# The copy of a relative bias to HBM, in one piece from GpSimd or head by head behind the weights

## The chip, the cores and the metric

One core of one Trainium2 chip. The metric is the device time of one execution in microseconds. Three runs of the kernel before gave 1661.22, 1663.39 and 1664.31 us; the profiled execution is a fourth one.

## What is computed

The reference is two layers of one kind of block, then one layer of another, on 256 tokens of width 1024, all in float32. A layer of the first kind is a mixer (windowed attention, dense attention and a gated branch), cross attention to a memory, and a feed-forward with a convolution over the tokens:

```
def conv_ffn(x, w_up, conv_k, conv_b, w_down):
    h = x @ w_up                                   # 1024 -> 2 * 2816
    h = sum(hp[:, j:j + S] * conv_k[j] for j in range(CONV_W)) + conv_b
    a, b = jnp.split(h, 2, axis=-1)
    return (jax.nn.gelu(a, approximate=False) * b) @ w_down
```

The second block's attention has 16 heads and adds to its scores a bias that depends on the distance of query and key alone, `bias_gr[:, :, t5_bucket(dist_w)]`. Its table is made early: for each head one row of 384 values over the distance, with a large negative number where the key lies ahead of the query.

## The kernel before

**Weights.** All weights lie in one stream in HBM, in the order of use. Each is multiplied as two parts of reduced precision: ScalarE rounds a raw piece into a buffer `wh` (L998), VectorE subtracts that from the raw piece and leaves the rest in `lows` (L1503), and TensorE makes three products of the parts (`run`, L478). Pieces of equal form are loaded two at a time, one group to a DMA: in the feed-forward a group is 128 partitions by 2048 values, 1 MB. The buffer `raw` is a ring of NR = 4 groups; `wh` has NH = 6 buffers, and the two casting engines go at most LA = 3 pieces ahead of the piece that is about to be multiplied. SyncE does nothing but issue these transfers (`sync`, L2354): before group gi it waits until TensorE has used group gi - 4. The queue of SyncE holds nothing else.

**The feed-forward.** There are NZ = 22 steps n. Step n takes two pieces, the features n and n + 22, which are one group: 24 matmuls of 128x256 each. ScalarE moves each product out of PSUM with scale and bias (L1243), VectorE adds the two neighbours of the convolution (L1833, L1836), ScalarE applies Gelu (L1225), GpSimd multiplies the halves (`e.tensor_tensor(hc...)`, L2275), ScalarE and VectorE split the product in two parts (L1228, L1823). Four PSUM banks go round among these products. Then the down-projection takes 22 pieces of 128x1024, 11 groups, 12 matmuls of 128x512 for each.

**The bias.** In layer 0 the selection matrix is loaded into `PT` once the cross attention has read `PT` for the last time (L1220). After feed-forward step 4 one matmul makes the table (L781), and VectorE adds the mask and writes `PT[0:16, 1024:1536]`, one head to a partition, in step 6 (L1842, signal `rel`). The copy to the scratch tensor `d_scr` [16, 128, 384] in HBM repeats each head's row 128 times, because the reader in the second block takes row p with an offset that shrinks by one from partition to partition (L2306). GpSimd issues the copy as one DMA behind its product of step 7 (L2278). The signal `bias_out` counts its end. In layer 1, `PT` is written again, by ScalarE (L1126) and VectorE (L1712), which wait for `bias_out`; GpSimd waits for it before it loads the table (L2304).

**Other DMAs.** GpSimd also loads parameters and gains; the 1.2 MB of parameters of layer 1 go out behind its last product of layer 0's feed-forward (L2281).

Of the kernel before, what the change touches and what calls it, by code (L numbers as in the profile page):

```python
# [231 lines left out]
def build(nc, wstream, specs_out, cst_d, rel_d, par_d, par2_d, x_d, xT_d, memT_d, lnp_d, scr_d, out_d, layout):  # L232
    with ExitStack() as ctx:

        def sb(name, f):
            return ctx.enter_context(nc.sbuf_tensor(name, [128, f], F32))
# [4 lines left out]
        def signal(name, step=1):  # L241
            s = Signal(ctx.enter_context(nc.semaphore("s_" + name)), step)
            signals.append(s)
            return s
# [8 lines left out]
        vec = signal("vec")  # L253
# [3 lines left out]
        cst_in, x_in, p2_in, rel_in, mem_in, bias_out, bias_in = (  # L257
            signal(n, 16) for n in ("cst", "x", "p2", "rel", "mem", "bias_out", "bias_in"))
# [16 lines left out]
        PT = sb("PT", 2048)  # L275
# [26 lines left out]
        def arena(n):  # L302
            o = at[0]
            at[0] += n
            assert at[0] <= ARENA
            return ar[:, o:o + n]
# [35 lines left out]
        def pr(name, p=128):  # L342
            o, n = layout["par"][0][name]
            return par[0:p, o:o + n]
# [16 lines left out]
        up = arena(RN * 259).rearrange("p (n t) -> p n t", t=259)  # L361
# [53 lines left out]
        pieces = Pieces()  # L415
# [32 lines left out]
        def unit(un):  # L448

            return un // 4, un // 2 % 2, un % 2, 4 * (un % 2)  # L450
# [536 lines left out]
        def scalar(e):  # L987
            w = Waits(e)
# [37 lines left out]
            for l in range(DEPTH):  # L1026
# [90 lines left out]
                def probs_copied(un):  # L1117
                    br, i, hh, hold = unit(un)
                    w.wait_ge(cross, "pT", l, un, 0)
                    if un < 2:  # L1120
                        if l:
                            w.wait_ge(bias_out)
                            w.wait_ge(cross, "xpv", l - 1, un)
                    else:
                        w.wait_ge(cross, "pv", l, un - 2)
                    e.copy(PTv[:, hold:hold + 2, :, :],  # L1126
                           A["pT", l, un, 0][:, :].rearrange("p (h k q) -> p h k q", h=2, k=2)).then_inc(*act.done("pT", l, un, 0))
# [124 lines left out]
                if l + 1 < DEPTH:  # L1252
# [3 lines left out]
                    n = pieces.of["kv", l + 1][-1] + 1  # L1256
# [16 lines left out]
            n = pieces.of["q2", 0][-1] + 1  # L1273
# [221 lines left out]
        def vector(e):  # L1495
            w = Waits(e)
# [57 lines left out]
            for l in range(DEPTH):  # L1554
# [148 lines left out]
                def probs_copied(un):  # L1703
                    br, i, hh, hold = unit(un)
                    w.wait_ge(cross, "pT", l, un, 1)
                    if un < 2:
                        if l:
                            w.wait_ge(bias_out)
                            w.wait_ge(cross, "xpv", l - 1, un)
                    else:  # L1710
                        w.wait_ge(cross, "pv", l, un - 2)
                    e.tensor_copy(PTv[:, hold + 2:hold + 4, :, :],  # L1712
                                  A["pT", l, un, 1][:, :].rearrange("p (h k q) -> p h k q", h=2, k=2)).then_inc(*vec.done("pT", l, un, 1))
# [112 lines left out]
                for n in range(NZ):  # L1826
                    for half in range(2):
                        m = n + half * NZ
                        lows_for("up", l, m)
                        h = hc[:, (2 * n + half) % 8, :]  # L1830
# [20 lines left out]
                if l + 1 < DEPTH:  # L1851
# [3 lines left out]
                    n = pieces.of["kv", l + 1][-1] + 1  # L1855
# [26 lines left out]
            n = pieces.of["q2", 0][-1] + 1  # L1882
# [135 lines left out]
            for i in range(2):  # L2018
# [4 lines left out]
                first = soff + 31  # L2023
# [160 lines left out]
        def gpsimd(e):  # L2184
            w = Waits(e)
# [10 lines left out]
            def scaled(tag, *ready):  # L2196

                w.wait_ge(*ready)
                for i in range(2):
                    e.tensor_scalar(xt(i), xt(i), ALPHA, None, ALU.mult).then_inc(*pool.done("scaled", *tag, i))  # L2200
# [23 lines left out]
            for l in range(DEPTH):  # L2224
                scaled((l, 1), *((x_in,) if l == 0 else (cross, "xT", 0, 3, 1, 1)))

                def rope_sin(br, i):
                    Xv = qk[:, i, 640 * br:640 * br + 640].rearrange("p (h s d) -> p h s d", s=2, d=32)
                    t2v = room[br][:, 640:1280].rearrange("p (h s d) -> p h s d", s=2, d=32)
                    n1 = rot[:, br, i, 32:64].unsqueeze(1).to_broadcast([128, 10, 32])  # L2230
                    if i:
                        w.wait_ge(vec, "rope", l, br, 0)
                    e.tensor_tensor(t2v[:, :, 0, :], Xv[:, :, 1, :], n1, ALU.mult).then_inc(*pool.done("sin", l, br, i))

                w.wait_ge(cst_in)
                if l:
                    for n in range(NZ - 4, NZ):
                        w.wait_ge(pool, "z", 0, n)
                        w.wait_ge(vec, "z", 0, n)
                for i in range(2):  # L2240
                    w.wait_ge(act, "q", l, 0, i)
                    w.wait_ge(act, "k", l, i)
                    rope_sin(0, i)
                for i in range(2):
                    w.wait_ge(vec, "vvar", l, i)
                    inverse_root(sm[:, 32 * i + 15:32 * i + 16], sm[:, 32 * i + 14:32 * i + 15]).then_inc(*pool.done("vrs", l, i))
                    w.wait_ge(vec, "qvar", l, i)
                    inverse_root(sm[:, 84:94], sm[:, 74:84], 10).then_inc(*pool.done("qrs", l, i))
                    if i == 0:
                        w.wait_ge(vec, "qg", l, 0)  # L2250
                        rope_sin(1, 0)
                    w.wait_ge(act, "vn", l, i)
                    w.wait_ge(par_in[l])
                    e.tensor_tensor(vt[:, i, :], vt[:, i, :], pr("clng"), ALU.mult).then_inc(*pool.done("vgain", l, i))
                    w.wait_ge(pool, "vgain", l, i)
                    e.tensor_tensor(vt[:, i, :], vt[:, i, :], pr("clnb"), ALU.add).then_inc(*pool.done("vn", l, i))
                w.wait_ge(vec, "qg", l, 1)
                rope_sin(1, 1)
                for kind, n, d in fills:
                    if kind == "merge" and n != 2:  # L2260
                        w.wait_ge(vec, "mul", l, n, d)
                        w.wait_ge(*((vec, "mul", l, 2, d) if n == 0 else (pool, "merged", l, 0, d)))
                        e.tensor_tensor(merged[:, d, :], merged[:, d, :], gates[:, gate_at[n] + d, :],  # L2263
                                        ALU.add).then_inc(*pool.done("merged", l, n, d))
                normed((l, 1))
                next_gains((l, 1), 3 * l + 1, (l, 2))
                scaled((l, 2), cross, "xT", l, 1, 1, 1)
                normed((l, 2))
                next_gains((l, 2), 3 * l + 2, (l, 3))
                scaled((l, 3), cross, "xT", l, 2, 1, 1)  # L2270
                for n in range(NZ):
                    s = 2 * n % 8
                    w.wait_ge(act, "ga", l, n)
                    w.wait_ge(vec, "conv", l, n + NZ)
                    e.tensor_tensor(hc[:, s, :], hc[:, s, :], hc[:, s + 1, :], ALU.mult).then_inc(*pool.done("z", l, n))  # L2275
                    if l == 0 and n == 7:
                        w.wait_ge(vec, "rel")
                        e.dma_start(scr_d, PT[0:16, 1024:1408].unsqueeze(1).to_broadcast([16, 128, 384])).then_inc(*bias_out.done())  # L2278
                if l == 0:
                    w.wait_ge(vec, "conv", 0, 2 * NZ - 1)  # L2280
                    e.dma_start(par, par_d[1]).then_inc(*par_in[1].done())  # L2281
                else:
                    for n in range(NZ - 4, NZ):
                        w.wait_ge(pool, "z", 1, n)
                        w.wait_ge(vec, "z", 1, n)
                    e.dma_start(grow, lnp_d[6][:, 0:1024]).then_inc(*gain_in[2, 1].done())
                normed((l, 3))
                if l == 0:
                    next_gains((0, 3), 3, (1, 1))
# [11 lines left out]
                w.wait_ge(product, "dn", 1, 1, 1)  # L2301

            rms((2, 1))
            w.wait_ge(bias_out)  # L2304
            first_block_done()
            e.dma_start(TB, bass.AP(scr_d.tensor, 127, [[383, 128], [128 * 384, 16], [1, 256]])).then_inc(*bias_in.done())  # L2306
            for i in range(2):
# [36 lines left out]

        def sync(e):
            w = Waits(e)
            for gi, (at, p, f) in enumerate(pieces.source):
                if gi >= NR:
                    for n in pieces.groups[gi - NR]:
                        w.wait_ge(product, "used", n)  # L2350
                elif gi:
                    w.wait_ge(xT_in[3])
                o = gi % NR * RAW
                e.dma_start(raws[0:p, o:o + f], bass.AP(wstream.tensor, at, [[f, p], [1, f]])).then_inc(*ring_in[gi % NR].done(gi))  # L2354
            w.wait_ge(out_done, 1, 1)


# [155 lines left out]
```

## Time and profile before

| | |
|---|---|
| median of three runs | 1663.39 us |
| profiled execution | 1660.03 us |
| its span | 1658.2 us |
| mean granted TensorE clock | 0.971 |
| TensorE busy (matmuls) | 1557.0 us, 94% |
| VectorE, ScalarE, GpSimd busy | 1028.6, 800.3, 246.6 us |
| DMA moved | 261.33 MB, mean 158 GB/s |
| the bias copy, one issue | 3072 KB, 37.0 us from issue to landing |
| a group of weights (196 issues) | 1024 KB, median 4.8 us from issue to landing |

Times in the views are counted from the first instruction. The share of the DMA queues is the time that their packets took, as a share of 16 engines over the stretch asked for. The queue q1 is SyncE's, with the weights; q10 is ScalarE's; q0 is GpSimd's, whose only transfer in flight from 374.3 to 411.3 us is the bias copy. PSUM is the memory that TensorE writes its products to.

### The profile page before, as it was taken

Reading aid. Unit: us, or ns where it says so; the run is one execution under the profiler, and the core shown is the slowest. Engines: PE = TensorE matmul, PEld = TensorE weight load, DVE = VectorE, ACT = ScalarE, POOL = GpSimd, SP = SyncE. Lnnn points to the kernel's source line nnn. Section 1 sums busy time; section 2 is a strip of 40 time slices with the busy share of each in tenths; the row PEclk is TensorE's granted clock in tenths of the full one; section 3 lists DMA queues with packets and bytes.
Section 4 is the critical chain, followed back from the end, with each engine's and each line's share of the span. In section 5 each row is a group of like instructions: output and inputs, shape, how many; then the busy total and the mean of one; then the engine's idle time right before and its main releaser. Section 6 shows DMA issues by size and latency. Waiting matters only on the chain.

```text
span 1658.2 us, 25362 instructions
## 1 busy us (share of the span) xinstructions
PE 1557.0 (94%) x10403; PEld 1401.7 (85%) x10403; DVE 1028.6 (62%) x1704; ACT 800.3 (48%) x1435; POOL 246.6 (15%) x225
## 2 busy tenths in 40 slices
PE   8999999898998999989989999899988799989999
PEld 6899888798986889988789986697876699979987
DVE  5764585675855575577677865445655486646643
ACT  4545445364642455444356652453445564435532
POOL 2300131211202130032031101003010041100000
PEclk9999999899999999999999999899999899989999
DMA  8523355359554533255345555455211244535543
GB/s 314 222 102 115 103 216 174 119 178 218 190 208 152 203 123 111 88 190 181 128 160 190 182 192 176 152 184 187 90 45 48 77 153 148 202 107 189 188 178 127
DMA packets 41027, 261.33 MB, mean 158 GB/s; under 512 B 4512, under 2 KB 5152, under 8 KB 14672
## 3 DMA queue, kind: packets, MB, share of 16 engines
q1 hardware_dynamic: 35600, 238.44, 41.5%
q0 software_dynamic: 2944, 15.69, 3.7%
q10 hardware_dynamic: 2368, 5.58, 0.9%
q8 instruction: 82, 1.34, 0.3%
q14 instruction: 33, 0.27, 0.0%
HBM read 254.98 MB, written 4.19 MB: 156 GB/s over the span
## 4 chain that ended last, share of the span: by engine, by line
PE 75%; DVE 11%; ACT 5%; issue 3%; DMA 3%; POOL 2%; ACTq 0%; DVEq 0%; POOLq 0%; SPq 0%
PE ps L478 67%; PE ps L581 3%; DMA raw<-d_wst 2%; DVE lows L1503 2%; POOL sm L2189 1%; PE ps L662 1%; ACT wh L998 1%; ACT S L1415 1%; DVE ar L2007 1%; DVE sm L1536 1%; DVE xs L1533 1%; PE ps L683 1%; DVE S L2069 1%; PE ps L577 1%; PE ps L701 0%
## 5 line engine op out<-in xcount | busy, mean ns | idle before, releaser
L1503 DVE TENSOR_TENSOR lows<-raw,wh 128x1024 fp32r<-128x1024 f32 (+3 forms) x473 | 546.1, 1174 | 261.3 <-ACT wh L998 258.5
L478 PE MATMUL ps<-xTr,wh 128*128 128x256 f32 (+2 forms) x3664 | 674.1, 286 | 17.0 <-DVE S L1833 7.5
L478 PEld LDWEIGHTS ps<-xTr,wh 128*128 128x128 f32 (+2 forms) x3664 | 574.7, 192 | 22.3 <-issue 14.2
L998 ACT CAST wh<-raw 128x1024 fp32r<-128x1024 f32 (+3 forms) x473 | 455.6, 989 | 176.1 <-DMA raw<-d_wst 164.4
L478 PE MATMUL ps<-xTr,lows 128*128 128x256 f32 (+2 forms) x1832 | 522.0, 285 | 0.0
L478 PEld LDWEIGHTS ps<-xTr,lows 128*128 128x128 f32 (+2 forms) x1832 | 352.4, 192 | 0.0
L478 PE MATMUL ps<-wh,arR 128*128 128x512 f32 x928 | 296.4, 398 | 4.1 <-DVE ar L1653 4.1
L478 PEld LDWEIGHTS ps<-wh,arR 128*128 128x128 f32 x928 | 175.1, 189 | 48.1 <-DVE ar L1653 5.8
L478 PE MATMUL ps<-lows,arR 128*128 128x512 f32 x464 | 184.1, 397 | 0.0
L478 PE MATMUL ps<-arR,wh 128*128 128x256 f32 (+1 forms) x832 | 147.2, 280 | 2.2 <-DVE lows L1503 2.2
L478 PE MATMUL ps<-wh,xTr 128*128 128x512 f32 x384 | 125.0, 405 | 12.2 <-DVE xTr L1522 6.7
L478 PEld LDWEIGHTS ps<-arR,wh 128*128 128x128 f32 (+1 forms) x832 | 126.7, 188 | 2.8 <-issue 2.6
L478 PE MATMUL ps<-arR,lows 128*128 128x256 f32 (+1 forms) x416 | 116.0, 279 | 0.0
L478 PEld LDWEIGHTS ps<-lows,arR 128*128 128x128 f32 x464 | 87.6, 189 | 20.6
L478 PEld LDWEIGHTS ps<-wh,xTr 128*128 128x128 f32 x384 | 75.6, 197 | 30.8 <-DVE xTr L1522 7.1
L2189 POOL TENSOR_TENSOR sm<-sm,cst 128x1 f32<-128x1 f32 (+3 forms) x27 | 42.3, 1566 | 384.4 <-DVE sm L1541 235.5
L478 PEld LDWEIGHTS ps<-arR,lows 128*128 128x128 f32 (+1 forms) x416 | 78.2, 188 | 0.0
L478 PE MATMUL ps<-lows,xTr 128*128 128x512 f32 x192 | 77.5, 404 | 0.0
L2275 POOL TENSOR_TENSOR S<-S 128x256 f32<-128x256 f32 x44 | 42.0, 955 | 222.8 <-ACT S L1225 201.0
L1243 ACT ACTIVATE S<-ps,ar 128x256 f32<-128x256 f32 x88 | 49.4, 562 | 51.1 <-PE ps L478 51.1
L2263 POOL TENSOR_TENSOR ar<-ar 128x256 f32<-128x256 f32 x32 | 31.9, 998 | 233.3 <-DVE ar L1653 233.1
L1415 ACT ACTIVATE S<-S,sm 128x128 f32<-128x128 f32 (+1 forms) x64 | 28.3, 443 | 56.6 <-DVE sm L2072 56.5
(265 smaller groups left out, 1554.0 us busy)
## 6 DMA issues: line engine op xcount, KB each, us to landing
raw<-d_wst SPq DMA_DIRECT2D x196, 1024.0 KB, 4.8
raw<-d_wst SPq DMA_DIRECT2D x24, 512.0 KB, 3.5
raw<-d_wst SPq DMA_DIRECT2D x12, 896.0 KB, 4.6
raw<-d_wst SPq DMA_DIRECT2D x8, 672.0 KB, 4.6
ar<-d_lnp POOLq DMA_DIRECT2D x5, 1024.0 KB, 5.2
raw<-d_wst SPq DMA_DIRECT2D x8, 441.0 KB, 3.4
d_scr<-PT POOLq DMA_DIRECT2D x1, 3072.0 KB, 37.0
ar<-d_par POOLq DMA_DIRECT2D x2, 1192.0 KB, 9.6
```

Of the source, the lines that this page charges most:

```text
L478: op = e.matmul(out, s, m, start=start and i == 0, stop=stop and i == len(pairs) - 1)
L577: e.matmul(b[:, :], ident, cst("wmask"), start=True, stop=True)
L581: op = e.transpose(o, x, ident[0:x.shape[0], 0:x.shape[0]])
L662: op = e.matmul(b[:, h * 64:(h + 1) * 64], PTv[:, hold + h, k, :], va[:, k, v:v + 64], start=(k == 0), stop=(k == 1))
L683: op = e.matmul(bv[:, k, :], qT[br][lo:lo + 64, 2 * hh + k, i * 128:(i + 1) * 128], kT[br][lo:lo + 64, :], start=True, stop=True)
L998: e.copy(high_of(m), raw_of(m)).then_inc(*high.done(m))
L1243: e.activation(hc[:, s, :], M["up", l, m][:, 0:T], ACT.Identity, bias=cb[:, m:m + 1], scale=ck[:, m, 1:2]).then_inc(*act.done("h", l, m))
L1415: op = e.activation(Sv[:, hold + h, 0:nk], Sv[:, hold + h, 0:nk], ACT.Exp, bias=nb[:, h:h + 1], scale=1.0, accum_out=su[:, h:h + 1])
L1503: e.tensor_tensor(low_of(m), raw_of(m), high_of(m).bitcast(F32), ALU.subtract).then_inc(*low.done(m))
L2189: return e.tensor_tensor(dst, src, mhalf[0:p, 0:n], ALU.pow)
L2263: e.tensor_tensor(merged[:, d, :], merged[:, d, :], gates[:, gate_at[n] + d, :], ALU.add).then_inc(*pool.done("merged", l, n, d))
L2275: e.tensor_tensor(hc[:, s, :], hc[:, s, :], hc[:, s + 1, :], ALU.mult).then_inc(*pool.done("z", l, n))
```

## The change

GpSimd's single copy is taken out. SyncE issues sixteen, one for each head, each from one partition of `PT` to 128 rows of `d_scr`. Part h goes out right behind the group of weights number first + h, where first is the group with feature 12 of layer 0's up-projection (feature 34 is in the same group). So parts 0 to 9 stand behind the groups of steps 12 to 21, parts 10 to 15 behind the first six groups of the down-projection. All are counted by one signal, and the three waits for it are for the last part. The wait for the table moves from GpSimd to SyncE.

```
--- before.py
+++ after.py
@@ -1119,7 +1119,7 @@ (and the same at 1705, and in gpsimd at 2301)
-                            w.wait_ge(bias_out)
+                            w.wait_ge(bias_out, 15)
@@ -2273,9 +2273,6 @@
                     e.tensor_tensor(hc[:, s, :], hc[:, s, :], hc[:, s + 1, :], ALU.mult).then_inc(*pool.done("z", l, n))
-                    if l == 0 and n == 7:
-                        w.wait_ge(vec, "rel")
-                        e.dma_start(scr_d, PT[0:16, 1024:1408].unsqueeze(1).to_broadcast([16, 128, 384])).then_inc(*bias_out.done())
@@ -2344,6 +2341,7 @@
         def sync(e):
             w = Waits(e)
+            first = pieces.home[pieces.of["up", 0, 12][0]][0]
@@ -2352,6 +2350,11 @@
                 e.dma_start(raws[0:p, o:o + f], bass.AP(wstream.tensor, at, [[f, p], [1, f]])).then_inc(*ring_in[gi % NR].done(gi))
+                h = gi - first
+                if 0 <= h < 16:
+                    w.wait_ge(vec, "rel")
+                    e.dma_start(scr_d[h:h + 1], PT[h:h + 1, 1024:1408].unsqueeze(1).to_broadcast([1, 128, 384])
+                                ).then_inc(*bias_out.done(h))
```

## Rows read from the trace of the kernel before

**Rows 1.** The page: header, TensorE's busy line, and the chain's shares by engine and line.

```profile
span 1658.2 us, 25362 instructions
...
PE 1557.0 (94%) x10403; PEld 1401.7 (85%) x10403; DVE 1028.6 (62%) x1704; ACT 800.3 (48%) x1435; POOL 246.6 (15%) x225
...
PE 75%; DVE 11%; ACT 5%; issue 3%; DMA 3%; POOL 2%; ACTq 0%; DVEq 0%; POOLq 0%; SPq 0%
PE ps L478 67%; PE ps L581 3%; DMA raw<-d_wst 2%; DVE lows L1503 2%; POOL sm L2189 1%; PE ps L662 1%; ACT wh L998 1%; ACT S L1415 1%; DVE ar L2007 1%; DVE sm L1536 1%; DVE xs L1533 1%; PE ps L683 1%; DVE S L2069 1%; PE ps L577 1%; PE ps L701 0%
```

**Rows 2.** Windows: stretch, busy time by engine, then clock, DMA share, GB/s.

```profile
374.00:411.00 37.00, 29.50 (x231) 29.58 (x231) 18.67 (x29) 14.70 (x25) 4.90 (x6) 0.91 0.98 204
420.00:457.00 37.00, 37.00 (x310) 37.00 (x310) 31.73 (x50) 24.14 (x40) 10.13 (x7) 1.00 0.53 182
```

**Rows 3.** Waits from 374 to 412: us in total, times, longest.

```profile
ACT wh L998 <- DMA raw<-d_wst: 15.4, 2, 12.7
PE ps L478 <- DVE S L1833: 7.5, 1, 7.5
```

**Rows 4.** The chain in order of time, 340 to 560: start, length, what.

```profile
378.49 21.91 DMA raw<-d_wst
```

**Rows 5.** The weights' issues and SyncE's queue, 420 to 457.

```profile
L2354 SPq DMA_DIRECT2D raw<-d_wst x6: 327/327/327, 422.6 to 451.4; - x6
...
DMA to landing us min/median/max: 4.7/4.9/5.0
...
q1 hardware_dynamic: 993, 7.22, 53.3%
```

**Rows 6.** Windows behind the stall.

```profile
403.20:407.60 4.40, 4.40 (x22) 4.40 (x21) 2.97 (x5) 1.82 (x3) 0.11 (x1) 0.51 1.03 243
407.60:412.00 4.40, 4.40 (x39) 4.40 (x38) 2.53 (x4) 2.99 (x5) 1.01 (x1) 1.00 0.98 379
```

**Rows 7.** The weights' issues in the down-projection, 470 to 512.

```profile
L2354 SPq DMA_DIRECT2D raw<-d_wst x7: 328/328/328, 474.0 to 507.6; - x7
```

**Rows 8.** Timelines of VectorE, GpSimd and ScalarE: start, length, instruction.

```profile
363.67 0.67 DVE L1842 TENSOR_TENSOR PT<-ps,PT 16x512 f32<-16x512 f32 x1
...
373.63 0.74 POOL L2275 TENSOR_TENSOR S<-S 128x256 f32<-128x256 f32 x1 [5.02 <-ACT S L1225]
374.32 1.10 POOL L2278 DMA_DIRECT2D d_scr<-PT  x1
...
608.96 0.59 ACT L1126 COPY PT<-ps 128x512 f32<-128x512 f32 x1 [1.72 <-PE ps L581]
```

**Rows 9.** GpSimd's DMA queue: packets, MB, share; 374:411, 378.4:392.4, 392.4:411.4.

```profile
GB/s 204 416 381 257 95 105 105 95 105 110 90 100 105 105 95 100 105 110 90 156 194 253 221 254 273 286 237 207 213 226 221 262 289 265 216 191 257 360 388 428
...
q0 software_dynamic: 704, 3.15, 69.0%
...
DMA packets 308, 1.44 MB, mean 103 GB/s; under 512 B 0, under 2 KB 0, under 8 KB 304
...
q0 software_dynamic: 304, 1.40, 95.7%
...
q0 software_dynamic: 344, 1.49, 55.4%
```

**Rows 10.** ScalarE's DMA queue, 1649 to 1652: the output.

```profile
q10 hardware_dynamic: 288, 0.52, 46.8%
```

**Rows 11.** GpSimd's DMA queue and its issue, 460 to 475.

```profile
q0 software_dynamic: 144, 1.22, 22.5%
...
ar<-d_par POOLq DMA_DIRECT2D x1, 1192.0 KB, 5.6
```

More of the change, by code:

```diff
@@ L1707, in probs_copied @@
                         if l:
-                            w.wait_ge(bias_out)
+                            w.wait_ge(bias_out, 15)
                             w.wait_ge(cross, "xpv", l - 1, un)
@@ L2303, in gpsimd @@
             rms((2, 1))
-            w.wait_ge(bias_out)
+            w.wait_ge(bias_out, 15)
             first_block_done()
```

## The prediction, made before the changed kernel ran

> **What bounds the kernel now.** I read the page first: its header and its busy line [rows 1]. TensorE is busy for 94% of the span, and the chain that ended last runs for 75% through it; the weights' DMA has 2% of that chain, some 33 us. So only two things can change the time: TensorE waiting for something, or TensorE at its lower clock. I then went to the stretch in which the bias copy is in flight, from 374.3 us, and compared it with a stretch of equal length behind it [rows 2]. In the undisturbed 37 us TensorE is busy all the time, the DMA engines 53%. In the copy's 37 us TensorE is busy for 29.5 us, at a mean clock of 0.91, and the DMA engines are at 98%. The waits of that stretch name the cause: ScalarE waited 15.4 us for raw weights, one wait of 12.7 us, and TensorE then stood 7.5 us for VectorE to free a PSUM bank [rows 3]. The chain shows the same from the other end: one transfer of weights, issued at 378.49, took 21.91 us and was the thing waited for [rows 4]. A transfer in the quiet stretch lands 4.9 us after its issue [rows 5]. Behind the stall the clock is low for 4.4 us: 22 matmuls ran at 0.51, where the next 4.4 us hold 39 at full clock [rows 6]. 22 of them at full clock would have taken 22 x 4.4 / 39 = 2.5 us, so 1.9 us went there. **The copy costs 7.5 + 1.9 = 9.4 us today**, and no more than that can be won.
>
> **What the weights' queue has to spare.** In the feed-forward of layer 0 SyncE issues one group of 1 MB as soon as TensorE has used the group four before it. In the up-projection the issues lie (451.4 - 422.6) / 5 = 5.76 us apart, in the down-projection (507.6 - 474.0) / 6 = 5.6 us [rows 5, 7]; at full clock TensorE sets that pace. The queue moved 7.22 MB in 53.3% of 37 us [rows 5], 2.73 us per MB or 2.9 us of all 16 engines for one group of 1.05 MB. So a part of the bias behind each group costs nothing as long as it holds the engines for less than 5.76 - 2.9 = 2.9 us (2.7 us in the down-projection).
>
> **Part by part.** *Taken away:* the wait for the table, one issue of 1.1 us on GpSimd [rows 8], and the copy's collision. GpSimd sat idle for 5 us before its product just before that issue, so the 1.1 us is worth nothing. The collision's 9.4 us are won, if nothing takes their place.
>
> *Added on SyncE:* 16 issues of about 0.33 us, as its other ones [rows 7]; it issues once per 5.6 us and otherwise waits. The new wait for the table comes ahead of the first part only. It stands behind the group of up-projection n = 12, which went out at 378.49, and the table was written at 363.7 [rows 8]: 14 us early, cost nothing. The three waits for the last part are in layer 1, at 609 us and later [rows 8]; the last part goes out behind the sixth down-projection group, near 500 us plus whatever the stretch gets longer, so they cost nothing as long as the stretch grows by less than some 100 us.
>
> *Added to the weights' queue:* sixteen parts of 0.197 MB, ten behind the groups of n = 12 to 21 and six behind down-projection groups. The next group of weights now stands behind a part in the same queue. What a part costs, the trace does not show; no transfer there reads a long block from one partition. The nearest rows: the copy took 69.0% of 37 us, 25.5 us of the engines for 3.15 MB from 16 partitions [rows 9]. Weights, over 128 partitions, cost 2.73 us per MB, the copy 8.1. So an eighth of the partitions made a megabyte 3.0 times as dear. The lower bound for a part is that it keeps the copy's price per byte, 25.5 / 16 = 1.6 us. The upper bound is that the price rises as the partitions fall, sixteenfold: 25.5 us a part. I take the trend between the two rows: three halvings of the partitions gave a factor 3.0, so four more give 3.0^(4/3) = 4.3, and a part 6.8 us. Within the copy there are two prices: alone on the engines 1.40 MB took 95.7% of 14 us, 9.6 us per MB; beside weights 1.49 MB took 55.4% of 19 us, 7.1 per MB [rows 9]. By the same trend these give 10.0 and 4.9 us a part. Parts will have weights queued before and behind them, so I shade 6.8 down to **6.4 us** and keep 4.9 and 10.0 as the forecast's ends.
>
> Why not a fast part? While the copy had the engines alone it moved a flat 103 GB/s with the engines 96% busy [rows 9], and it writes to HBM. Writes to HBM are not what is slow: the output's, from 128 partitions, moved 0.52 MB in 46.8% of 3 us, over 370 GB/s [rows 10]. So the source side, few partitions, is what is slow, and a part has one partition where the copy had sixteen.
>
> *The sum.* A group with its part needs 2.9 + 6.4 = 9.3 us. Ten groups fall behind by 9.3 - 5.76 = 3.54 us each, 35.4; six by 9.3 - 5.6 = 3.7 us each, 22.2. The parameters of layer 1 are loaded at the end of the up-projection, 22.5% of 15 us = 3.4 us of engines [rows 11], hidden now and not in a full queue: together 61.0 us. The ring absorbs some: the transfer of rows 4 landed 21.9 - 4.9 = 17.0 us late and TensorE stood 7.5 us, so 9.5 us are covered. That leaves 51.5 us of standing; minus the 9.4 us won, **+42.1 us**. The five down-projection groups behind the parts lose nothing more, for the queue needs 2.9 us of their 5.6. The lower clock after each standing adds nothing in my sum: 24 matmuls at the slow rate of 4.4 / 22 = 0.2 us, twice over, are 9.6 us for a group, about the 9.3 that DMA needs. It can add 0.3 us a group, 5 us.
>
> The profiled execution took 1660.03 us; the median of the runs is 1663.39, 3.4 us above it. 1660.0 + 42.1 + 3.4 = **1705.5 us**.
>
> The rule weighed against this: the Trainium skill, SBUF — State Buffer, "Door 1: The DMA port swizzle", says that DMA bandwidth depends on how many of 16 ports the partitions reach, about 27.2 GB/s each, four neighbouring partitions sharing one: partitions 0 to 15 reach four ports, one partition a single one. The trace agrees for the copy: 103 GB/s flat against 109. By that page a part would take 0.197 MB / 27.2 GB/s = 7.2 us, and the sum would come to 1718 us.
>
> **The rivals.**
> 1. *Groups of four partitions share a way out.* The flat 103 GB/s would be four ways of 25.8, and a part, having one way, takes 7.6 us with all 16 engines queued at it. Then the lags are 10 x 4.74 + 6 x 4.9 + 3.4 = 80.2, minus 9.5 and 9.4: +61.3, 1725 us. For it: how flat the rate is. Against: the second half of the copy, in which other engines carried weights while some waited, so a part may be partly hidden. This is the page's rule above at the row's rate. Chance 0.27.
> 2. *A part is cheap, and the change is faster.* If the copy was slow because of how it was laid over the engines (sixteen regions of HBM written at once, say) and not because of its source, a part costs 1.6 us, 2.9 + 1.6 = 4.5 is below 5.6, TensorE never stands and the 9.4 us are won: 1654 us. It decides as soon as a part is below 2.9 us; the break-even with the won 9.4 us is where 10 x (b - 2.86) + 6 x (b - 2.7) + 3.4 = 18.9, b = 3.8 us. Against: the output's writes are fast. Chance 0.15.
> 3. *Part on one engine.* If a part is not spread, one engine moves 0.197 MB, three times its 65.5 KB share of a group, 3 x 2.9 = 8.6 us, and each group is as late as that engine: lags of 57.4 + 35.4 + 3.4, +77, 1741 us. Chance 0.07.
> 4. *The price rises with each partition lost*, 25.5 us a part: lags of 226 + 137 + 3, some +347, over 2000 us; the waits of layer 1 then bind too. Chance 0.03.
> 5. *It comes out even*, near b = 3.8 us: 1663 us. Also here: the change does not do what it says, the parts pile up somewhere else and cost about what they cost today. Chance 0.03.
>
> **How the numbers follow.** Forecast (a part between 4.9 and 10.0 us, mostly near 6.4): 0.45, rival 1: 0.27. With 4.9 us the sum is 33.6 + 3.4 - 18.9 = +18, 1682 us; with 10.0 us +100, 1763 us, for parts that never overlap with weights. Forecast and rivals 1 and 3 hold 0.79; a range from 1670 to 1750 us holds nearly all of them and something of rival 5. Left out are rivals 2 and 4 and the last of the tail. About 0.2% (3.3 us) is what a measurement of this kernel can tell from no change. Faster by more: 0.15, rival 2 alone. Within: 0.03. Slower: 0.82.
>
> **What would show it.** Right: sixteen issues of 192 KB behind the groups; no standing near 395 us, TensorE's first stop instead at the group of n = 15 (three parts late by 3.54 us each are past the 9.5), near 413 us; from there until past 520 us the DMA engines over 95% busy at only 1.25 MB per 9.3 us, 134 GB/s; weights landing 15 us or more after issue; ScalarE waiting for raw in nearly every group, TensorE busy some 60% and at times at the lower clock. A part's price is the distance of two issues of weights there minus 2.9 us. Wrong: the issues stay 5.76 us apart, the engines 75% busy and TensorE gapless through the feed-forward: then a part was cheap (rival 2). If the distance is 11 us and one engine carries the parts, it was rival 3. If the stretch behaves as I say but the time elsewhere moves too, the ring's 9.5 us or the layer 1 waits were misjudged.

## The result, and the profile after

| | before | after |
|---|---|---|
| median | 1662.24 us (8 runs) | 1666.68 us (8 runs) |
| ratio, 95% interval | | 1.003 [1.0017, 1.0044] |
| profiled execution, its span | 1660.03, 1658.2 us | 1666.77, 1665.0 us |

The change makes the kernel 4.4 us slower. The direction was forecast, the size was not: 1705.5 us, and the range began at 1670.

The page of the kernel after: the header, two DMA queues (packets, MB, share of 16 engines), and the issue line of the parts (count, KB each, median us to landing).

```profile
span 1665.0 us, 25377 instructions
...
q1 hardware_dynamic: 37904, 241.59, 44.7%
q0 software_dynamic: 2240, 12.55, 2.1%
...
d_scr<-PT SPq DMA_DIRECT2D x16, 192.0 KB, 17.7
```

The sixteen parts are there, in the weights' queue. To see what they cost, the chain in order of time is the best view, for it shows the piece from the table's matmul to the end of the down-projection. First the kernel after, then the kernel before.

```profile
349.77 63.57 PE ps L478 x528
413.37 0.03 issue
413.40 17.03 DMA raw<-d_wst
...
439.34 19.86 DMA raw<-d_wst
...
462.50 54.94 PE ps L478 x228
517.44 0.03 issue
```

```profile
349.42 29.01 PE ps L478 x240
...
403.19 109.20 PE ps L478 x669
512.39 0.03 issue
```

Before, the piece lasts 512.39 - 349.42 = 163.0 us, after, 517.44 - 349.77 = 167.7. The rest of the difference between the two spans lies outside this piece and is no more than runs of one kernel differ by. The one transfer waited for before [rows 4] has gone; two others stand in the chain, later.

The waits of the kernel after, from 374 to 560 us and, for ScalarE, to 545 (us in total, times, longest), beside [rows 3]:

```profile
PE ps L478 <- DVE S L1836: 5.5, 2, 3.3
PE ps L478 <- DVE lows L1503: 3.8, 5, 1.3
```

```profile
ACT wh L998 <- DMA raw<-d_wst: 50.4, 18, 5.0
```

One stop of 7.5 us became seven short ones, 9.3 us in all. (The waits for the attention behind the feed-forward, 6.7 us for L1522, are the same in both kernels and are left out.) The windows (stretch, busy time by engine, clock, DMA share, GB/s) say where, beside [rows 2]:

```profile
374.00:411.00 37.00, 37.00 (x310) 37.00 (x309) 28.43 (x45) 22.35 (x38) 5.70 (x7) 1.00 0.93 183
411.00:440.00 29.00, 26.72 (x216) 25.84 (x215) 18.09 (x28) 13.97 (x24) 4.00 (x4) 1.00 0.93 184
440.00:470.00 30.00, 22.37 (x130) 18.68 (x129) 18.52 (x27) 14.88 (x24) 4.27 (x5) 0.89 0.94 197
...
460.00:465.00 5.00, 2.50 (x6) 2.02 (x7) 2.96 (x5) 3.06 (x8) 2.27 (x3) 0.50 0.97 209
```

The old collision is repaired: 37.00 of 37 us busy where it had been 29.50. The DMA engines stay at 93% and the queue falls behind slowly; TensorE first stops at 425 us. In the 7.5 us from 455.0 it stands for 5.5, and the clock is then at 0.50, its lower level of 1.2 GHz.

How fast the queue falls behind is read from issues and landings. SyncE's timeline (start, length, instruction), then, in us after the issue, the landing of the weights issued at 378.84, 390.36, 396.12, 413.40, 419.25, 439.34, 445.93 and 473.40:

```profile
378.84 0.33 SPq L2352 DMA_DIRECT2D raw<-d_wst  x1
...
384.98 1.90 SPq L2356 DMA_DIRECT2D d_scr<-PT  x1
...
413.40 1.84 SPq L2352 DMA_DIRECT2D raw<-d_wst  x1
415.29 3.87 SPq L2356 DMA_DIRECT2D d_scr<-PT  x1
419.25 3.60 SPq L2352 DMA_DIRECT2D raw<-d_wst  x1
...
473.40 0.33 SPq L2352 DMA_DIRECT2D raw<-d_wst  x1
```

```profile
DMA to landing us min/median/max: 7.0/7.0/7.0
...
DMA to landing us min/median/max: 11.2/11.2/11.2
...
DMA to landing us min/median/max: 11.3/11.3/11.3
...
DMA to landing us min/median/max: 17.0/17.0/17.0
...
DMA to landing us min/median/max: 17.8/17.8/17.8
...
DMA to landing us min/median/max: 19.9/19.9/19.9
...
DMA to landing us min/median/max: 16.6/16.6/16.6
...
DMA to landing us min/median/max: 9.0/9.0/9.0
```

The first of these landed at 385.8, the last at 482.4 us, fourteen groups later: **6.9 us for a group and its part**. I had summed 9.3.

The 6.9 is a mean of two kinds. The groups issued at 396.12, 419.25 and 445.93 stand between parts 3 and 4, 7 and 8, 11 and 12. They landed 5.9, 6.6 and 3.3 us after the group ahead of them, and the last group 5.1; the ten others landed 7.0 to 8.1 us after the one ahead, 7.6 in the mean. So the queue is quicker where the next part's partition lies in the next four, which the experiments explain.

One view shows the part by itself, while the packets of the next group of weights have not started: the queue from 378.9 to 381.2 us.

```profile
DMA packets 41, 0.06 MB, mean 27 GB/s; under 512 B 0, under 2 KB 41, under 8 KB 41
...
q1 hardware_dynamic: 41, 0.06, 93.9%
```

27 GB/s with the engines 94% busy: a part alone takes 0.197 MB / 27 GB/s = 7.3 us. So alone it is slower than my 6.4, and yet group and part together need no more than about the part alone, where the two added up would be 10.2. The experiments take these two numbers apart.

### The profile page after: what moved, and what is told of

Same layout as the page of the kernel before. It is cut to its first block, busy times and chain, and to the rows that moved or that the text cites. A ratio compares the mean times of both kernels' runs of the same rounds, so it can differ in the third digit from the quotient of the medians.

```text
span 1665.0 us, 25377 instructions
## 1 busy us (share of the span) xinstructions
PE 1563.3 (94%) x10403; PEld 1404.8 (84%) x10403; DVE 1029.7 (62%) x1704; ACT 800.5 (48%) x1435; POOL 241.1 (14%) x224
## 4 chain that ended last, share of the span: by engine, by line
PE 75%; DVE 11%; ACT 4%; DMA 4%; issue 3%; POOL 2%; ACTq 0%; DVEq 0%; POOLq 0%; SPq 0%
PE ps L478 66%; DMA raw<-d_wst 3%; PE ps L581 3%; DVE lows L1503 2%; PE ps L662 1%; POOL sm L2189 1%; ACT wh L998 1%; ACT S L1415 1%; PE ps L683 1%; DVE ar L2007 1%; DVE sm L1536 1%; DVE xs L1533 1%; DVE S L2069 1%; PE ps L577 1%; PE ps L701 0%
## 5 line engine op out<-in xcount | busy, mean ns | idle before, releaser
L478 PEld LDWEIGHTS ps<-xTr,wh 128*128 128x128 f32 (+2 forms) x3664 | 573.7, 192 | 19.5 <-issue 11.4
L2275 POOL TENSOR_TENSOR S<-S 128x256 f32<-128x256 f32 x44 | 37.7, 858 | 230.8 <-ACT S L1225 230.8
L1415 ACT ACTIVATE S<-S,sm 128x128 f32<-128x128 f32 (+1 forms) x64 | 28.3, 443 | 56.5 <-DVE sm L2072 56.4
```

The source lines that it names most:

```text
L478: op = e.matmul(out, s, m, start=start and i == 0, stop=stop and i == len(pairs) - 1)
L1415: op = e.activation(Sv[:, hold + h, 0:nk], Sv[:, hold + h, 0:nk], ACT.Exp, bias=nb[:, h:h + 1], scale=1.0, accum_out=su[:, h:h + 1])
```

## The experiments

Theory P: four neighbouring partitions share one way out, of about 27 GB/s, and a part with one head has one. Its rivals: the number of partitions counts, wherever they lie (C); the number of blocks put into the weights' queue counts (D). All diffs are against the kernel after; each run's ratio is to the kernel before, run on the same chip.

**e1: no copy.**

```
-                h = gi - first
-                if 0 <= h < 16: ...   (the part's DMA)
-            w.wait_ge(bias_out, 15)   (three times)
-   bass.AP(scr_d.tensor, 127, ...)
+   bass.AP(wstream.tensor, 127, ...)
```

> The copy is left out altogether, and the second block reads its bias from the weights' tensor, so the attention there works on other numbers. This is the ceiling. If the copy cost 9.4 us before (7.5 us of standing, 1.9 us of slow clock), this runs 9.4 us faster than the kernel before, about 1653 us. If part of what happened behind the copy was caused by something else, the gain is smaller, and then so is the loss that the sixteen parts cause (14 us against this kernel by my count).

Measured: 1653.64 us, ratio 0.9949 [0.9936, 0.9963]. The chain has the whole piece in one:

```profile
349.49 153.43 PE ps L478 x1053
```

153.4 us against 163.0 and 167.7: the copy cost 9.5 us before and costs 14.2 us after. My count of 9.4 for what the change could win was right. The windows of the whole piece, after and here, divide the 14.2:

```profile
349.77:517.44 167.67, 157.75 (x1055) 144.02 (x1055) 105.85 (x146) 83.81 (x126) 16.97 (x20) 0.98 0.81 196
...
349.49:502.92 153.43, 153.43 (x1054) 142.69 (x1055) 105.57 (x146) 83.61 (x126) 14.59 (x20) 1.00 0.56 193
```

For the same matmuls TensorE is busy 157.8 us against 153.4, so 4.3 us are matmuls at the lower clock; 9.9 us are idle, 9.3 of them in the seven waits.

**e2: parts of eight rows of all heads.**

```
-    e.dma_start(scr_d[h:h + 1], PT[h:h + 1, 1024:1408].unsqueeze(1).to_broadcast([1, 128, 384])
+    r = slice(8 * h, 8 * h + 8)
+    e.dma_start(scr_d[:, r], PT[0:16, 1024:1408].unsqueeze(1).to_broadcast([16, 8, 384])
```

> Sixteen parts behind the same groups, the same bytes and the same 128 blocks of 1.5 KB in each, but each part holds eight rows of all sixteen heads, so it reads 16 partitions. Theory P (a source's partitions share ways out of about 27 GB/s each, four neighbours to one way): four ways, a part takes 1.8 to 2.3 us instead of 7, 2.9 + 2.3 is below 5.6, everything is hidden: 1653 us, equal to e1. Rival D (what costs is the number of blocks in the weights' queue, 128 more per group): as the changed kernel, 1667 us, landings of weights again 7 us apart.

Measured: 1653.19 us, ratio 0.9946 [0.9934, 0.9958], the time without any copy. From 372 to 474 us the weights landed so:

```profile
DMA to landing us min/median/max: 4.8/5.2/6.9
```

As many blocks and bytes as in the kernel after, in the same queue at the same places: D is out.

**e3 and e4: four heads, near and far.**

```
+    a, r = h // 4, slice(32 * (h % 4), 32 * (h % 4) + 32)
e3:  e.dma_start(scr_d[4 * a:4 * a + 4, r], PT[4 * a:4 * a + 4, 1024:1408] ... [4, 32, 384]
e4:  e.dma_start(scr_d[a:16:4, r],          PT[a:16:4, 1024:1408]          ... [4, 32, 384]
```

> Each part holds 32 rows of four heads in neighbouring partitions (0 to 3, 4 to 7, ...). Theory P: one way out as with one head, 7.2 us for a part, so no better than the changed kernel: 1667 us or more (it may also be laid on fewer engines, which makes it no faster). Rival C (the price falls with the number of partitions, wherever they lie, by the trend of my prediction): four partitions are 2.1 times as fast as one, the weights keep up, 1653 to 1656 us.

> As e3, but the four heads of a part lie four partitions apart (0, 4, 8, 12 and so on). Theory P: four ways out, 1.8 us for a part, hidden: 1653 us, clearly below e3. Rival C: equal to e3, whatever that is. Rival D: both as the changed kernel, 1667 us.

Measured: e3 1681.99 us, ratio 1.0119 [1.0106, 1.0132]; e4 1652.9 us, ratio 0.9944 [0.9931, 0.9956]. The two differ in nothing but which four heads a part holds, and they lie 29 us apart. This is the experiment that decides for P against C. One thing moves along in every run here: a head is both a partition of `PT` and a region of `d_scr`, so no run changes the source and leaves the place of writing. Against the place of writing as the cause speaks the output, whose 256 KB pieces go into a stretch of 512 KB at over 370 GB/s [rows 10]. The windows from 380 to 470 us, e3 and then e4, and e3's packets in that stretch:

```profile
380.00:470.00 90.00, 75.82 (x574) 72.48 (x573) 53.80 (x83) 43.07 (x71) 10.58 (x12) 0.96 0.56 170
```

```profile
380.00:470.00 90.00, 90.00 (x663) 85.69 (x662) 66.52 (x96) 53.50 (x84) 10.69 (x15) 1.00 0.67 233
```

```profile
DMA packets 3259, 15.32 MB, mean 170 GB/s; under 512 B 241, under 2 KB 1659, under 8 KB 1659
```

e3 falls behind further than the kernel after, at a DMA share of only 0.56. Its 1659 - 241 = 1418 blocks of 1.5 KB in 90 us are 24 GB/s, 8.1 us for a part. Ten groups at 8.1 - 5.76 and six at 8.1 - 5.6, minus 9.5, are 28.9 us; e3 is 28.3 us slower than e1. So again the way out sets the pace, and here it runs a little slower than the 27 of a one-head part. Why is open. The low share fits a part that lies on a few of the engines, whose weights then wait for all of it. The Trainium skill, DMA: Bandwidth & Descriptors, "Why a DMA increments its semaphore by 16 and not by 1", says that a transfer is spread over the largest number of engines up to 16 that divides the slowest dimension of both its sides, here 4 (in e4 too, where nothing was lost). The mean share is in line with it, but no view here shows single engines.

**e5 and e6: the same parts, more spread out.** e5 puts a whole part behind every second group, e6 half a part (64 rows) behind each of 32 groups.

```
e5:  if 0 <= h < 32 and h % 2 == 0:   h //= 2
e6:  if 0 <= h < 32:   a, r = h // 2, slice(64 * (h % 2), 64 * (h % 2) + 64)
                       e.dma_start(scr_d[a:a + 1, r], PT[a:a + 1, 1024:1408] ... [1, 64, 384]
```

> The changed kernel's parts, one head each, but behind every second group of weights, so 32 groups carry sixteen parts. The table's last reader is then later, but still ahead of layer 1's write at 609 us. Theory P: two groups and one part need 2 x 2.9 + 7.2 = 13.0 us if nothing overlaps against 11.5 us of TensorE's work, and 9.8 us or less if a part costs what it did in the changed kernel (6.9 us for a group with its part, so 4.0 us for the part). So: 1653 us, as without the copy, if weights move beside a part; by strict addition 1.5 us behind per pair, 16 pairs 24 us, minus the 9.5 that the ring covers, 1667 us.

> 32 half parts (64 rows of one head) behind 32 groups in a row: the same bytes per time from one partition as in e5, but evenly. A half part alone takes 3.6 us. If a part and weights add up strictly, a group needs 2.9 + 3.6 = 6.5 us against 5.76, 0.8 behind for each of the first 21 groups, some 15 us, 9.5 of them covered: 1659 us. If weights move beside a part, 2.9 + 2.0 = 4.9 us, hidden: 1653 us.

Measured: e5 1653.01 us, ratio 0.994 [0.9928, 0.9952]; e6 1653.41 us, ratio 0.9942 [0.993, 0.9954]. Neither shows the 1667 and 1659 us of strict addition. One way out at 27 GB/s is enough if the copy has 11.5 us for each head; the kernel after gives it 5.76, and a part needs about 7.

**e7: one piece, from SyncE.**

```
+    if gi == first:
+        e.dma_start(scr_d, PT[0:16, 1024:1408].unsqueeze(1).to_broadcast([16, 128, 384]))...
```

> The copy in one piece as before (16 partitions, 3 MB), but issued by SyncE behind the group of step 12, in the weights' own queue. Theory P: four ways out of 27 GB/s are 29 us, and the next group of weights stands behind all of it, some 26 us late where it was 17.0 us late before: TensorE stands about 16 us instead of 7.5, 1670 us. If the queue it goes through makes no difference and only the bytes count: as before, 1662 us.

Measured: 1670.66 us, ratio 1.0048 [1.0035, 1.006]. The chain, then the wait:

```profile
378.88 32.22 DMA raw<-d_wst
```

```profile
PE ps L478 <- DVE S L1833: 17.8, 1, 17.8
```

The weights landed 32.2 - 4.9 = 27.3 us late and TensorE stood 17.8: the ring covered 9.5 us, to a tenth as in [rows 3, 4]. So the cover was read rightly. Of the two ways to send the one piece, from the same moment on, a queue of its own is the milder.

**e8: the parts in GpSimd's queue.**

```
 (gpsimd, behind the product of step n, layer 0)
+    if l == 0 and n >= 7:
+        h = n - 7
+        e.dma_start(scr_d[h:h + 1], PT[h:h + 1, 1024:1408] ... [1, 128, 384])   (h = 15 behind the loop)
```

> The sixteen one-head parts, but issued by GpSimd behind its products of steps 7 to 21, the sixteenth right behind the fifteenth, so the parts have a queue of their own and the weights' queue is as before. Theory P: the way out of one partition is what is short, so the parts take 7.2 us each and overlap each other; the weights can pass them where an engine takes turns between queues. If turns are taken freely: 1653 us. If an engine that holds blocks of a part is held up whatever the queue, as in the 14 us of rows 9 in which no weights moved: as the changed kernel, 1667 us.

Measured: 1683.18 us, ratio 1.012 [1.0105, 1.0136], worse than either expectation. From 380 to 470 us:

```profile
q0 software_dynamic: 828, 2.54, 62.1%
q1 hardware_dynamic: 1859, 13.55, 35.8%
```

The parts hold the engines for 55.9 of 90 us, about 13 parts at 4.3 us. A queue of their own does not let the weights pass freely. Why it is 16 us worse than the same parts in the weights' queue is not settled. Two differences show: a packet holds 3.1 KB (2.54 MB in 828) where it held 1.5, and GpSimd's issues take it 0.55 us each to the end, where SyncE was held for up to 3.95.

**e9: two parts behind each of eight groups.**

```
-    h = gi - first
+    for h in (2 * (gi - first), 2 * (gi - first) + 1):
```

> The same sixteen one-head parts, two behind each of the first eight groups. What is open is why a group with its part needed 6.9 us in the changed kernel and not 2.9 + 7.2. Theory S (the one way out is busy all the time, weights move beside it on the engines that do not wait for it): two parts need 13.8 us, the group is hidden in it, so each of eight groups falls 8.0 us behind, 64 us, minus 9.5, plus some 5 of slow clock: 60 us above the kernel without the copy, 1713 us. Rival F (a part holds the engines for a fixed 4.0 us): 2.9 + 8.0 = 10.9 us, 5.1 behind eight times, 41 - 9.5 + 5: 1690 us. Strict addition at 7.2: 17.3 us, 92 - 9.5 + 5: 1741 us.

Measured: 1715.01 us, ratio 1.0317 [1.0299, 1.0335], within 2 us of theory S. SyncE's timeline:

```profile
389.21 3.09 SPq L2352 DMA_DIRECT2D raw<-d_wst  x1
392.34 11.33 SPq L2356 DMA_DIRECT2D d_scr<-PT  x2
...
404.41 12.38 SPq L2356 DMA_DIRECT2D d_scr<-PT  x2
...
460.06 0.61 SPq L2352 DMA_DIRECT2D raw<-d_wst  x1
```

From one of these issues of weights to the other are five groups, (460.06 - 389.21) / 5 = 14.2 us for one group and two parts, 7.1 us a part, 27.7 GB/s. The 2.9 us of the weights have vanished in it: the way out is what the time follows, and the weights run beside it. The expectation's total is right and its split is not. The piece, in one window, is 61.0 us longer than e1's:

```profile
350.60:565.04 214.44, 168.60 (x1055) 156.25 (x1055) 105.51 (x146) 83.61 (x126) 18.43 (x20) 0.87 0.75 153
```

Of the 61.0, TensorE stands 45.8 us, not 54.5, and 15.2 are the lower clock, not 5. What the queue falls behind by, less the cover, is 8 x (14.2 - 5.76) - 9.5 = 58.0 us either way; a TensorE that is slowed down waits the less for it.

**e10: the same parts, in another order.**

```
+    p = 4 * (h % 4) + h // 4
-    e.dma_start(scr_d[h:h + 1], PT[h:h + 1, ...
+    e.dma_start(scr_d[p:p + 1], PT[p:p + 1, ...
```

> The changed kernel with the heads in another order: 0, 4, 8, 12, 1, 5, 9, 13 and so on, so that two parts behind each other never lie in the same four partitions. One part still has one way out. Theory S: engines that are through with a part go on to the next group and the next part, which leaves by another way, so the ways are no longer full all the time and the loss of the changed kernel shrinks or goes: 1653 to 1660 us. Rival (every part stands in the queue for itself, engines in step): the order makes no difference, 1667 us.

Measured: 1653.43 us, ratio 0.9953 [0.994, 0.9965]. The chain, and the windows from 380 to 470 us, beside those of the kernel after in the same stretch:

```profile
351.71 153.43 PE ps L478 x1053
```

```profile
380.00:470.00 90.00, 90.00 (x670) 86.05 (x670) 65.83 (x97) 52.65 (x84) 11.23 (x15) 1.00 0.95 218
```

```profile
380.00:470.00 90.00, 80.08 (x601) 75.52 (x600) 60.23 (x90) 47.58 (x78) 13.00 (x15) 0.96 0.93 187
```

153.43 us again, to a hundredth the piece of the kernel without a copy. Only the order of the heads differs from the kernel after. So two parts in a row are in flight together, and in heads' order they press through the same way. The landings of the kernel after say the same, quicker wherever two parts in a row lay in different fours. Note that the DMA share is higher here than in the kernel after, 0.95 against 0.93, and nothing is lost: a busy DMA engine can be one that waits.

## Why the prediction was right or wrong

**What could be won: right.** 9.4 us forecast, 9.5 by e1's chain, 8.8 by the medians of e1 and of the kernel before beside it.

**What the ring covers: right.** 9.5 us, confirmed by e7.

**The place of the first part: wrong, without effect.** I had the group of step 12 go out at 378.49; it goes out at 373.1, one group earlier, and the transfer of [rows 4] was step 13's. The table was still 9 us early (written at 364), so the wait cost nothing, as said. The layer 1 waits cost nothing either: the last part was issued at 473.8 us and landed 12.5 us later.

**A part's price: the step that failed.** I took 6.4 us, with ends at 4.9 and 10.0, and added it to 2.9 us of weights: 9.3 us a group. The trace shows 6.9, so a part adds 4.0. Two errors lie in it. The smaller: the trend over the number of partitions was the wrong law. Which four partitions, not how many, sets the rate (e3 against e4); the 16 of the copy had four ways, one head has one, and the price alone is 7.3 us. Rival 1 had it at 7.6, and the rule of the Trainium skill that the prediction sets beside it (SBUF — State Buffer, "Door 1: The DMA port swizzle") at 7.2. The larger, common to my sum and to rival 1: I let the part and the weights follow each other on all engines in step. Had I used 7.6 us as rival 1 did, I would have been further off. They overlap. As I read it, engines that are through with their share of a part move weights while the others still press through the way out; no view shows single engines. The cost of a group with its part is about the longer of the two, 7.6 us where the next part leaves by the same way and 6.9 in the mean, not their sum, which e9 shows at twice the load. My own rows had a hint of it, the copy's lower price beside weights [rows 9], and I used it to shade a number instead of asking what it would become when the way out is full.

**The sum with that term put right.** Ten groups at 6.9 - 5.76 and six at 6.9 - 5.6 are 11.4 + 7.8 = 19.2 us behind, minus 9.5: 9.7 us of standing. Measured are 9.3. That it comes so near is partly luck. The last group that TensorE waited for is the twelfth of the sixteen, issued at 439.34 and landed at 459.2, some 18 us after the same group in e1 (issued at 436.16, landed 5.1 us later); the lag of the four behind it was not waited for. And in e3 and e9 the same sum, 28.9 and 58.0, is near the whole loss of the piece with the slow clock in it (61.0 in e9), where here it is near the standing alone. The load of layer 1's parameters needs no term of its own: it falls into the stretch over which 6.9 was averaged.

**The slow clock: mis-sized.** I put nothing for it, at most 5 us. The piece lost 14.2 us: 9.9 idle, and 4.3 of matmuls at the lower clock, near the upper end of what I allowed. My reason for nothing was that the slow matmuls run within the time that the DMA needs anyway; e9 bears that out, the kernel after does not. Together 14.2 - 9.5 = +4.7 us in the chain, +4.4 in the medians.

**The alternatives.** Rival 2, a cheap part, came out in e2 and e4 at 1653 us, with the same bytes sent from several ways out; for one-head parts it was wrong. Rival 3, one engine for a part, fails on the 94% at which a part alone held the engines, and rival 4's 25.5 us on the 7.3. The break-even at 3.8 us was near the truth in an uncomfortable way: the part's 4.0 us sat just on the losing side of it, and only 0.03 of my chance lay there. That the direction came out right is therefore close to luck.

**What beats both kernels.** e2, e4, e5, e6 and e10 all run at 1653 us, 9 us below the kernel before and 13 below the kernel after, with the whole reference computed. e10's edit is as small as any: one line more, and p for h in the next.

## What to carry to other kernels

A small transfer is not cheap because it has few bytes: ask how many ways out of the on-chip memory its source partitions have, and cut a copy so that each part, or at least each two in a row, reaches several. The number of partitions alone is no guide: e3's cut, four neighbours, was the worst of those with one part to a group. When two kinds of transfer meet in a queue, compare the longer of their limits with the time at hand before adding them up (e5, e6 and e9 follow the longer one). Work out the break-even price of the unknown term first; when it lies inside the bounds, the chances have to say so.

## What was not expected of the hardware

SyncE's issue of a transfer, 0.33 us when the queue is short, took up to 3.95 us in the kernel after and 12.38 us for a pair in e9: it seems that with enough queued the issuing engine itself is held, and so is all that stands behind it. In the kernel before, the DMA engines did not take turns freely between two queues either: 0.02 MB of weights moved in the 14 us after 378.4 in which the copy filled the engines and three groups of weights were issued in the other queue.

```profile
q1 hardware_dynamic: 3, 0.02, 0.4%
```

A queue of its own did not help the small parts (e8). And the rate of one way out lies between 24 and 28 GB/s by five roads: 27 alone, 27.7 in e9, 24 in e3, a quarter of 103 in [rows 9], and a quarter of the 100 GB/s at which e7's piece ran.
